# Half of a gather moved between the gate/up matmuls, a first gather in two parts, and more filler matmuls in the router's hole

## What is computed

```python
def hier_moe(x, w_grp, b_grp, w_rt, b_rt, w_gate, w_up, w_down):
    # top-1 group of 4, then top-2 of its 4 experts: a gate per token and expert
    ...
    gate = (jax.nn.one_hot(g_idx, N_GROUPS)[:, :, None] * within[:, None, :]).reshape(T, N_EXPERTS)
    h = jax.nn.silu(jnp.einsum("td,edf->tef", xt, w_gate)) * jnp.einsum("td,edf->tef", xt, w_up)
    y = jnp.einsum("tef,efd->td", h * gate[:, :, None], w_down)

h = h + mixer(rmsnorm(h, norm_mix[i]))          # pooling in layer 0, attention in layer 1
h = h + hier_moe(rmsnorm(h, norm_ffn[i]), ...)  # 16 experts, D=2048, F=512
```

## Time and profile before

| | |
|---|---|
| time, median of 3 runs | 1395.6 us (1393.68 to 1396.21) |
| time of the profiled execution | 1394.36 us |
| its span, first to last instruction | 1392.6 us |
| PE busy | 1343.2 us, 96% of the span |
| DVE, ACT, POOL busy | 555.4, 424.9, 42.2 us |
| mean granted TensorE clock | 0.992 of full |
| read from HBM | 478.56 MB, mean 345 GB/s |

### The profile page before, as it was taken

One profiled execution on the slowest core, in us unless ns is written; L12 is line 12 of the kernel. 1 busy time (PEld: TensorE's weight loads), 2 busy tenths in 40 slices (PEclk: granted clock), 3 DMA queues, 4 the chain that ended last, 5 costly groups with the idle time before them and its releaser, 6 DMA issues.

```text
span 1392.6 us, 21931 instructions
## 1 busy us (share of the span) xinstructions
PE 1343.2 (96%) x9113; PEld 767.8 (55%) x9113; DVE 555.4 (40%) x902; ACT 424.9 (31%) x644; POOL 42.2 (3%) x35
## 2 busy tenths in 40 slices
PE   9899999999999999999999999999999999899998
PEld 8534444443334458888888877764444444334434
DVE  6813223132222246566665665551322313222223
ACT  5511111120101136665656565531111111111112
POOL 1200000000000000000000000110000000000000
PEclk9999999999999999999999999999999999999999
DMA  9999999999999999544545444569999999999996
GB/s 357 403 415 421 425 393 428 428 429 428 429 427 426 425 391 375 185 167 154 180 137 194 152 151 154 179 246 417 421 427 387 428 427 429 428 429 426 427 425 264
DMA packets 78010, 481.69 MB, mean 346 GB/s; under 512 B 5502, under 2 KB 5712, under 8 KB 47476
## 3 DMA queue, kind: packets, MB, share of 16 engines
q1 hardware_dynamic: 77348, 477.50, 85.0%
q10 hardware_dynamic: 432, 2.65, 0.5%
q0 software_dynamic: 160, 0.52, 0.1%
HBM read 478.56 MB, written 2.10 MB: 345 GB/s over the span
## 4 chain that ended last, share of the span: by engine, by line
issue 53%; PE 30%; DMA 11%; DVE 3%; POOL 1%; ACT 1%; SPq 0%; ACTq 0%; POOLq 0%; DVEq 0%
PE ps L1738 13%; DMA ring<-in_moe_w_up 10%; PE ps L1555 7%; PE ps L1786 4%; PE ps L1636 2%; PE ps L1698 1%; POOL head_rs L618 1%; DVE ws L1008 1%; PE ps L1699 1%; DMA resid<-in_x 1%; PE ps L1798 1%; PE ps L1769 0%; DVE ps L1312 0%; DVE resid L1315 0%; PE ps L1576 0%
## 5 line engine op out<-in xcount | busy, mean ns | idle before, releaser
L1738 PE MATMUL ps<-ring,xg 128*64 128x512 f32 x1920 | 441.0, 601 | 28.8 <-DMA ring<-in_moe_w_up 25.9
L1555 PE MATMUL ps<-ws,xs 128*128 128x512 f32 x1632 | 382.2, 392 | 2.6 <-DVE ws L1011 1.1
L1555 PEld LDWEIGHTS ps<-ws,xs 128*128 128x128 f32 x1632 | 302.9, 188 | 70.3 <-DVE ws L1011 3.5
L1738 PEld LDWEIGHTS ps<-ring,xg 128*64 128x64 f32 x1920 | 140.7, 138 | 297.4 <-issue 297.3
L1786 PE MATMUL ps<-ring,hidT 128*64 128x512 f32 x896 | 198.8, 595 | 0.0
L1011 DVE SCALAR_TENSOR_TENSOR ws<-ring,vecs,ws 128x512 fp32r<-128x512 f32 x192 | 134.3, 747 | 87.4 <-ACT ws L639 87.4
L1193 DVE TENSOR_TENSOR y_lo<-ps,y_hi 64x512 fp32r<-64x512 f32 x112 | 77.1, 689 | 191.6 <-ACT y_hi L701 189.0
L639 ACT ACTIVATE ws<-ring,vecs 128x512 fp32r<-128x512 f32 x192 | 127.3, 715 | 82.9 <-PE ps L1555 82.9
L1171 DVE TENSOR_TENSOR resid<-resid,ps 128x512 f32<-128x512 f32 x112 | 71.9, 684 | 169.9 <-PE ps L1699 169.9
L701 ACT ACTIVATE y_hi<-ps 64x512 fp32r<-64x512 f32 x112 | 66.3, 592 | 209.2 <-PE ps L1786 207.2
L1786 PEld LDWEIGHTS ps<-ring,hidT 128*64 128x64 f32 x896 | 61.9, 137 | 113.3 <-issue 111.9
(11 more groups left out here) (184 smaller groups left out, 767.5 us busy)
## 6 DMA issues: line engine op xcount, KB each, us to landing
ring<-in_moe_w_gate SPq DMA_DIRECT2D x46, 2048.0 KB, 15.7
ring<-in_moe_w_up SPq DMA_DIRECT2D x46, 2048.0 KB, 20.1
ring<-in_moe_w_down SPq DMA_DIRECT2D x44, 2048.0 KB, 18.0
ring<-in_moe_w_down SPq DMA_DIRECT2D x32, 1024.0 KB, 15.5
ring<-in_w_kv SPq DMA_DIRECT2D x32, 1024.0 KB, 5.7
ring<-in_moe_w_gate SPq DMA_DIRECT2D x26, 1024.0 KB, 14.8
ring<-in_moe_w_up SPq DMA_DIRECT2D x26, 1024.0 KB, 14.4
ring<-in_w_q SPq DMA_DIRECT2D x16, 1024.0 KB, 5.3
```

The source lines that it names most:

```text
L1555: last = mm(ps[:, bank + t, :], xs[:, px, k, cols], ws[:, b, pw, j, :], start=(first and j == 0 and n == 0), stop=(last_unit and j == 1 an ...
L1738: last = mm(ps[CAP * h:CAP * h + CAP, b, :], xg[:, b, k, :], both[h][:, j, :], start=(k == 0), stop=(k == KD - 1))
```

## The change

Five edits, three of them on PE:

1. In b = 1 of every pair but the last, the first half of the next pair's gather (tiles 0 to 7, 48 matmuls) stands between quarter 1 and quarter 2 of gate/up; in the hole behind quarter 3 only tiles 8 to 10 are left (18 matmuls).
2. The first gather of a layer is cut: tiles 0 to 7 stand ahead of quarter 0, tiles 8 to 15 behind it.
3. `WARM_ROUTE` goes from 8 to 16, `WARM_PICK` from 5 to 6: 32 and 12 fillers in place of 16 and 10.
4. On DVE the second `tokens_half` of the first gather goes behind the operations that make the gates and the scales' input.
5. The router's matmuls wait for ACT's half of `xr` before their first two and for DVE's half before their last two, in place of for both at the start.

```diff
-        WARM_START, WARM_BANDS, WARM_ROUTE, WARM_PICK, WARM_UNITS = 56, 16, 8, 5, 4
+        WARM_START, WARM_BANDS, WARM_ROUTE, WARM_PICK, WARM_UNITS = 56, 16, 16, 6, 4
@@ DVE, moe
-                tokens_half(G0 + 1, 0, 1)
                 step(nc.vector.tensor_tensor(HOT2[:, :, 1:5, :], HOT2[:, :, 1:5, :], wide(W2[:, :, 1:5], NG), ALU.mult))
...
                 make_side(0)
+                tokens_half(G0 + 1, 0, 1)
                 scales_out(G0 + 1, 0, FIRST_SCALES)
@@ PE, route_block
-                pe.wait_ge(xr_act, NBLK * l + c + 1)
-                pe.wait_ge(xr_dve, NBLK * l + c + 1)
...
                 for j in range(4):
+                    if j % 2 == 0:
+                        pe.wait_ge((xr_act, xr_dve)[j // 2], NBLK * l + c + 1)
@@ PE, moe
-                gather(0, range(KD))
+                gather(0, range(KD // 2))
@@ PE, pair: behind quarter q of expert b
+                            if b == 1 and q == 1 and not last_pair:
+                                pe.wait_ge(pick_done, PICKS + i + 2)
+                                gather(0, range(KD // 2))
...
+                            if b == 0 and before is None and q == 0:
+                                gather(0, range(KD // 2, KD))
@@ PE, pair: behind quarter 3
                         if b == 1 and not last_pair:
-                            pe.wait_ge(pick_done, PICKS + i + 2)
                             pe.wait_ge(side_done, PICKS + i + 2)
                         if not (b and last_pair):
                             gather_scales(1 - b)
-                            gather(1 - b, range(TURN_AT))
+                            gather(1 - b, range(KD // 2 if b else 0, TURN_AT))
                             pe.wait_ge(slot_scale_done, XG + 2 * i + b + 2)
```

## The result

| | before | after |
|---|---|---|
| time, median (range), 6 runs each | 1394.64 us (1392.17 to 1397.41) | 1406.43 us (1401.99 to 1413.07) |
| ratio, 95% interval | | 1.0091 (1.0062 to 1.0121) |
| time and span of the profiled execution | 1394.36, 1392.6 us | 1406.13, 1404.3 us |

The account below looks back on a forecast made before the run. PE was taken to bound each layer's first stage, the loads the rest. Insertions 5.3, start 0 and fillers 0.1 us gave +5.4 on 1394.4, so 1399.8, and 1401.0 us as median; eight-in-ten range 1397.0 to 1404.0.

Parts of the forecast that it names:

- What bounds the kernel: In each layer's experts, PE sets the time first, for some 120 us, then the loads do.
- the dry spell: Loads fall to 164 GB/s until PE ends quarter 1 of pair 2's first expert; shifts there move the layer one to one.
- The inserted half gather: Between gate/up quarters of second experts: 1.33 us of PE each, 5.3 us for four; the other ten free.
- my upper bound of 1.57: Highest price in us of one inserted half gather: nothing comes back and a matmul costs 32.7 ns.
- The clock in the emptied holes: Rival, 8%: the clock falls in second experts' holes, 1.5 to 1.7 us each; all four in first stages: 1408 us.
- The start: First gather in two parts plus added fillers: zero for both layers together, with -1.3 to +1.2 us as ends.
- The router's two waits: Router matmuls waiting separately for the halves of `xr`: gain taken as 0, between 0 and 0.3 us per layer.
- The sum: Whole kernel: 5.3 us for insertions, 0 for the layers' starts, 0.1 for fillers, +5.4 us in all, giving 1401.0 us.

Follow-up runs that it names:

- four early insertions: Kernel before with the half gather inserted only in second experts of pairs 0 and 1: 1403.97 us, ratio 1.0071.
- ten late ones: Kernel before with the half gather inserted only in second experts of pairs 2 to 6: 1393.97 us, ratio 1.0002.
- with the code moved: Changed kernel without the inserted half gathers, 12 start fillers left out so later PE code moves 24 instructions: 1394.73 us, ratio 1.0012 against before.

## Why the prediction was wrong, point by point

**What bounds the kernel: right, and shown.** The four early insertions cost +9.9 us, the ten late ones 0.3, all of them 9.2. The stretch between the two layers' first stages is 752.0 to 753.0 us in every kernel. PE decides up to the dry spell and the loads behind it.

**The inserted half gather: right in kind, the price too low.** "One insertion costs 1.47 - 0.14 = 1.33 us of PE" failed. Stage 1 of a layer holds two insertions and goes, in layer 1, from 115.80 to 119.02: 1.61 us each, just above my upper bound of 1.57. The matmuls themselves take 1.50 us; the quarters around them lose 0.15 us more, since the four quarters with their insertion are 15.39 us in place of 13.74 (149.51 to 164.90 in the changed kernel; before, 1014.77 to 1028.51 by the same marks); and 0.05 come back in place of 0.14, because the last six matmuls take 0.28 us after the idle stretch, not 0.18. The row of before that goes with it:

```profile
1014.77 13.90 PE L1738 MATMUL ps<-ring,xg 128*64 128x512 f32 x64
```

Four insertions are 6.4 us, not 5.3. The 25 ns per matmul of the Trainium skill, "TensorE: Matmul & The Clock Gate", section "Back-to-back issue gap", would have been further off: 48 took 1.50 us in this trace, 31 ns each.

**The clock in the emptied holes: the rival that I gave 8% is in the sum.** I argued that the first expert's idle 1.14 us went without a fall. One hole was no sample: over the fourteen traces that same first hole of both layers has a fall behind it in 4 of 28 (a fall counts when it starts within 2 us behind the turning of `hid`). The emptied holes, idle 1.2 us, have one behind 16 of 56 (five kernels); filled with fillers, behind 0 of 28; with 1.81 us idle, behind 10 of 14; and the same second experts' holes with their old 66 matmuls, behind 0 of 98. One fall costs 1.67 to 1.70 us in the first stage, and nothing visible in the second. Four traced kernels have idle holes at the four early places, and there were 4 falls in these 16. By that, one fall in an execution (an estimate), 6.4 + 1.7 = 8.1 us for edit 1; measured 9.2 (7.4 to 11.0) and 9.9. The changed kernel's trace had one such fall, and another behind the very first expert, whose hole is as before. That idle time brings the falls is shown by the counts. That they are all of the rest is not shown: filling the holes gave 4 us in the changed kernel and 1 in the kernel with edit 1 alone, both by ratios whose intervals overlap.

**The start: "I take zero for both layers together" failed, twice.** First, I measured against a first gather at half the clock, from one execution. In layer 1 that was chance: the two kernels with an uncut first gather and no fall have 115.80 us there, the kernel before 117.34. And I had the layers the wrong way round. I counted fully on the fillers in layer 1 and by half in layer 0, but the clock is at 0.50 during layer 0's first gather in all seven traces with the old fillers and in one of the seven with the new ones, during layer 1's in two of seven and none. What the fillers give back, they give mostly in layer 0. Against a full clock the cut gather loses 1.18 us, of which 0.85 are PE's wait for the first half of the tokens; for the rest, 0.33, my reading is that PE changes twice more between the two kinds of matmul. So the fillers' gain and the cut's loss are separate: -1.5 and +2.6 us alone. Second, the end of the layer: edits 2 to 5 cost 3.9 and 3.8 us, but 1.7 with the code moved, against 1.1 as the sum of the parts. The 2.2 us between 3.9 and 1.7 go with the second stall of PE in the first code behind the loop and with the clock that stays down around it: the stretch that holds them is 348.16 and 347.70 us, moved 345.40. The falls of the clock in the first stages, which the moved kernel's trace doesn't have, and the 12 fillers fewer at the start can have a share, and what starts the stall isn't shown.

**The router's two waits (edit 5):** not tried alone. By the traces it brings 0.1 us: from the last matmul ahead of the router's second half (L1576) to the first of L1609 it is 2.16 to 2.17 us in layer 1 in the six kernels with it and 2.28 in the eight without, in layer 0 2.98 to 3.14 in both kinds. It was forecast at 0, with 0 to 0.3 as ends.

**The sum.** Edit 1 +9.2 and edits 2 to 5 +3.9 make 13.1, the whole change +12.7 (8.6 to 16.9 by its interval; 11.8 by the medians). My sum had 5.3, 0 and 0.1. Three of its steps failed: an insertion is 1.61 us of PE and not 1.33 (6.4 in place of 5.3); the falls of the clock behind the emptied holes, which I kept out of the sum as a rival of 8%, are some 1.7 us; and the start, taken at zero, is 3.9 with the code where the change puts it. These make 12.0. My 1401.0 us comes out in one execution of six, the fastest with 1401.99 us; it has a granted clock of 0.997 where the others have 0.989 to 0.990, so what I had taken as the rule, a clock that hardly falls, was the exception. What stays open is why two of the six needed 1411.5 and 1413.1 at the same granted clock as one of 1405.7.

## What to carry to other kernels

Before moving filler out of a hole, ask what the hole waits for: here a chain of ACT and DVE hangs on the quarter's end, so the filler was free there, and moved to a place where PE decides it cost its full length (1.50 us) and a little more. Where two resources take turns as the bound, find the last moment at which the one waits for the other; the same edit cost 2.5 us per pair ahead of it (9.9 for four) and nothing that the runs can tell behind it. Take the clock of a stretch from several traces before counting on it, and when a kernel with a small edit is slower without a reason, move its code by a few instructions and time it again.

## What the runs showed of the hardware

- Behind an idle stretch of PE of 1.2 us in these holes the clock fell to 1.2 GHz at times (16 of 56), behind one of 1.8 us mostly (10 of 14), behind the same holes without idle time never (0 of 98, and 0 of 28 with fillers). A fall cost 1.7 us where PE decides.
- PE stalled 2.1 to 3.9 us in the first matmuls behind the loop while the loads ran at 420 GB/s. The length of the stalls went with where the code lay: with 24 instructions fewer ahead of it, edits 2 to 5 cost 2.2 us less. That code is being loaded is my reading of this; the profile calls the idle time "issue", and the small transfers of the instruction queues that are in flight (three in 8 us) are there as well in the kernel before, which has no such stall at this place.
- A block of 64-column bf16 matmuls between float32 matmuls cost some 0.15 us beside its own time (15.39 us in place of 13.74 + 1.50).
